# Decoder layer with a 16-expert mixture: expert gating ahead of two transposes, a 128-row scatter, low parts stored in the raw weight slots, four expert blocks loaded among the dense ones

## The reference

```python
for e in range(N_EXPERTS):
    a = jax.nn.silu(h @ w_gate[e]) * (h @ w_up[e])
    out = out + gates[..., e:e + 1] * (a @ w_down[e])
```

## Time and profile before

| | before |
|---|---|
| median of 3 runs | 578.33 us |
| profiled execution, first to last instruction (span) | 576.9 us |
| TensorE (PE) busy | 563.2 us, 98% |
| VectorE busy | 276.5 us, 48% |
| ScalarE busy | 234.9 us, 41% |
| dense part (to the first expert matmul) | 0 to 358.2 us |
| experts | 358.2 to 570.2 us |
| moved by DMA | 165.2 MB, 286 GB/s in the mean |

### The profile page before, as it was taken

One profiled execution on the slowest core, in us unless ns is written; L12 is line 12 of the kernel. 1 busy time (PEld: TensorE's weight loads), 2 busy tenths in 40 slices (PEclk: granted clock), 3 DMA queues, 4 the chain that ended last, 5 costly groups with the idle time before them and its releaser, 6 DMA issues.

```text
span 576.9 us, 7293 instructions
## 1 busy us (share of the span) xinstructions
PE 563.2 (98%) x2875; PEld 379.4 (66%) x2875; DVE 276.5 (48%) x415; ACT 234.9 (41%) x314; POOL 20.8 (4%) x15
## 2 busy tenths in 40 slices
PE   8999999999998999999999999999999999999995
PEld 7889888888876778888888786434444434443333
DVE  4463686976588653997765627311222221220002
ACT  6664673584594555833655643211111111111112
POOL 0000000050010000000100120000000000000000
PEclk9999999999999999999999999999999999999998
DMA  8994674566633338656656798999999999999962
GB/s 306 406 302 151 217 258 147 196 252 208 219 110 110 110 103 310 240 157 213 198 167 198 282 427 348 351 425 425 426 428 425 427 425 426 427 425 427 425 282 75
DMA packets 46300, 165.19 MB, mean 286 GB/s; under 512 B 4276, under 2 KB 5432, under 8 KB 33720
## 3 DMA queue, kind: packets, MB, share of 16 engines
q1 hardware_dynamic: 43872, 159.12, 71.8%
q10 hardware_dynamic: 2392, 5.59, 2.8%
HBM read 163.63 MB, written 1.06 MB: 285 GB/s over the span
## 4 chain that ended last, share of the span: by engine, by line
PE 90%; DVE 3%; ACT 2%; DMA 1%; DVEq 1%; issue 1%; POOL 0%; SPq 0%
PE ps L2010 19%; PE ps L1562 15%; PE ps L1554 15%; PE ps L1555 15%; PE ps L2029 10%; PE ps L1535 5%; PE ps L2054 3%; PE ps L1926 3%; DMA w_raw<-in_w_in 1%; PE ps L1729 1%; PE ps L1703 1%; PE ps L1840 1%; PE ps L1863 1%; PE ps L1917 1%; PE ps L1617 1%
## 5 line engine op out<-in xcount | busy, mean ns | idle before, releaser
L969 DVE TENSOR_TENSOR w_lo<-w_raw,w_hi 128x2048 fp32r<-128x2048 f32 (+2 forms) x52 | 113.9, 2208 | 58.9 <-ACT w_hi L565 58.3
L1554 PE MATMUL ps<-w_hi,act_hi 128*128 128x512 f32 (+1 forms) x288 | 112.2, 392 | 0.0
L1555 PE MATMUL ps<-w_hi,act_lo 128*128 128x512 f32 (+1 forms) x288 | 110.1, 384 | 0.0
L565 ACT ACTIVATE w_hi<-w_raw 128x2048 fp32r<-128x2048 f32 (+2 forms) x52 | 95.3, 1852 | 30.3 <-PE ps L1562 25.2
L2010 PE MATMUL ps<-e_raw,xg 128*64 128x512 f32 x400 | 89.1, 596 | 0.0
L1562 PE MATMUL ps<-w_lo,act_hi 128*128 128x512 f32 (+1 forms) x288 | 70.3, 386 | 0.0
L2010 PEld LDWEIGHTS ps<-e_raw,xg 128*64 128x64 f32 x400 | 27.4, 137 | 53.4 <-issue 53.2
L1554 PEld LDWEIGHTS ps<-w_hi,act_hi 128*128 128x128 f32 x288 | 54.1, 188 | 10.9 <-issue 0.7
L1555 PEld LDWEIGHTS ps<-w_hi,act_lo 128*128 128x128 f32 x288 | 54.1, 188 | 10.0
L1562 PEld LDWEIGHTS ps<-w_lo,act_hi 128*128 128x128 f32 x288 | 52.6, 188 | 10.9 <-issue 0.7
L884 ACT ACTIVATE gu<-ps,rs_slot 128x512 f32<-128x512 f32 x16 | 11.0, 687 | 96.2 <-PE ps L2010 96.2
(11 more groups left out here) (292 smaller groups left out, 710.6 us busy)
## 6 DMA issues: line engine op xcount, KB each, us to landing
w_raw<-in_w_in SPq DMA_DIRECT2D x30, 1024.0 KB, 5.2
e_raw<-in_w_expert_gate SPq DMA_DIRECT2D x25, 1024.0 KB, 15.1
e_raw<-in_w_expert_up SPq DMA_DIRECT2D x25, 1024.0 KB, 18.0
e_raw<-in_w_expert_down SPq DMA_DIRECT2D x22, 1024.0 KB, 20.9
w_raw<-in_w_expert_down SPq DMA_DIRECT2D x10, 1024.0 KB, 22.5
w_raw<-in_w_expert_gate SPq DMA_DIRECT2D x7, 1024.0 KB, 13.2
w_raw<-in_w_expert_up SPq DMA_DIRECT2D x7, 1024.0 KB, 16.2
w_raw<-in_w_xkv SPq DMA_DIRECT2D x4, 1024.0 KB, 5.1
```

Of the source, the lines that this page charges most:

```text
L565: A(bview(w_hi, b, blocks[b].shape), bview(w_raw, b, blocks[b].shape), ACT.Copy).then_inc(hi_done, 1)
L969: V.tensor_tensor(bview(w_lo, b, sh), bview(w_raw, b, sh), f32(bview(w_hi, b, sh)), ALU.subtract).then_inc(lo_done, 1)
L1554: MM(o, xh[:, t0 + k, i * P:(i + 1) * P], wh[:, k], start=first and k == 0, stop=False)
L1555: MM(o, xl[:, t0 + k, i * P:(i + 1) * P], wh[:, k], start=False, stop=False)
```

## The change

Four edits.

1. **Low parts over raw blocks.** `w_lo` has no memory of its own any more: it is written over the raw block in its slot. So the load of block b has to wait until TensorE has used block b-4.
2. **Four expert blocks early.** The 32 KB for each partition that this frees become four slots `e_early`; expert blocks 0 to 3 are loaded behind dense blocks 10 to 13.
3. **Gating ahead of the transposes.** The host writes gate and up weights in a new order, as four blocks of 1 MB for each expert, so that one PSUM bank holds gate in its left 256 columns and up in its right 256, for both halves of the tokens' columns. ScalarE applies silu to the left half (with the token's scale), VectorE multiplies by the right half, and TensorE makes two transposes in place of four; VectorE then copies the result to `a_st`.
4. **Scatter over 128 rows.** High and low part of one column half lie in one tile (`y_side`), so 4 matmuls over 128 rows take the place of 8 over 64. ScalarE and VectorE make them in two instructions each, of 64 partitions. The last expert scatters as before.

```diff
-        w_lo_at = place["at"]
-        w_lo = sb("w_lo", [P, RING, BLK], f32r)
+        w_lo = at("w_lo", w_raw_at, [P, RING, BLK], f32r)
+        e_early = sb("e_early", [P, RING, BLK])
...
                 if b >= RING:
-                    sp.wait_ge(hi_done, split_count(b - RING))
-                    sp.wait_ge(lo_done, split_count(b - RING))
+                    sp.wait_ge(mm_done, b - RING + 1)
...
             for b in range(8, NB1):
                 weight_block(b)
+                if b in EARLY:
+                    expert_load(b - EARLY[0])
...
-            for n in range(NB2):
+            for n in range(RING, NB2):
...
-                    A(y_hi[:], ps[:, 3, :], ACT.Copy, scale=w_).then_inc(s["y_hi_done"], 1)
+                    for w in range(2):
+                        A(y_side[w][side(w)], ps[side(w), 3, :], ACT.Copy, scale=w_[side(w)]).then_inc(s["y_hi_done"], 1)
...
             def gate_silu(r, e):
-                act.wait_ge(s["gu_turned"], r * NE + (e + 1))
-                A(e_act[:], ps[:, 2, :].rearrange("p (k w c) -> p k w c", w=2, c=SLOTS)[:, :, 0], ACT.Silu).then_inc(s["gate_silu_done"], 1)
...
+                A(e_act[:], ps[:, 0, 0:FF // 2], ACT.Silu, scale=rs_slot[g % 2][:, j:j + 1]).then_inc(s["gate_silu_done"], 1)
...
+                V.scalar_tensor_tensor(a_tok[:], ps[:, 0, FF // 2:FF], rs_slot[e // EPG % 2][:, e % EPG:e % EPG + 1], e_act[:],
+                                       ALU.mult, ALU.mult).then_inc(s["gu_moved"], 1)
...
+                V.tensor_copy(a_st[:].rearrange("p k c -> p (k c)"), ps[:, 2, 0:FF // 2]).then_inc(s["a_ready"], 1)
...
-                for f in range(FF // P):
-                    ins = turn(ps[:, 2, f * P:(f + 1) * P], gu[:, f:FF:FF // P], P)
+                for c in range(2):
+                    ins = turn(ps[:, 2, c * P:(c + 1) * P], a_tok[:, c * P:(c + 1) * P], P)
...
-                        for y in (y_hi, y_lo):
+                        if n is None:
                             for w in range(2):
...
+                                ins = MM(ps[:, 4 + 2 * i + w, :], selT[g % 2][:, j, i * P:(i + 1) * P], y_side[w][:], start=False,
+                                         stop=False, skip_group_check=True)
```

More of the change, by code:

```diff
@@ L49 @@
 E_RING, E_FIRST = 16, 18
+EARLY = range(10, 14)
 W_HI_ORDER = (2, 3, 0, 1)
@@ L157, in build_program @@
         m_at = region(POST + 8192)
[L158 removed]
+        assert not any(v % LINE for v in (w_hi_at, w_raw_at, act_at, q_at, zq_at, zo_at, zqk_at, zv_at, zg_at, tg_at, m_at))
         zif_at = region(NT * 8 * 4)
@@ L353, in build_program @@
             if e < NE:
-                expert_block += [(e, which, half) for half in range(2) for which in ("gate", "up")]
+                expert_block += [(e, "gu", q) for q in range(4)]
             if e:
@@ L359, in build_program, with used @@
         assert NB2 % E_RING == 0
-        def used(e, which, half):
-            return NB1 + block_at[e, which, half] + 1
+        def used(e, which, part):
+            return NB1 + block_at[e, which, part] + 1
         def split_count(b):
@@ L441, in e_slot @@
             turns = n // ring + 1 + (len(range(k, NB2, E_FIRST)) if later else 0)
[L442 to L446, removed]
+            earlier = list(EARLY_LANDED.values()) + [0] * (8 - RING) + list(LOADED.values())
+            before_ = earlier[k] if k < len(earlier) else 0
+            return e_raw[k], e_in_slot[k], before_ + 16 * turns
         SCATTERS = 2 * NE + 3
@@ L501, in _, with expert_load @@
                  (router_b[:], d_in["router_b"].rearrange("(o n) -> o n", o=1).to_broadcast([P, NE])))
+            def expert_load(n, later=False):
+                e, which, part = expert_block[n]
+                raw, landed, _ = e_slot(n, later)
+                if which == "gu":
+                    sp.dma_start(raw[:, :], d_in["w_gate_up"][e, part]).then_inc(landed, 16)
+                else:
+                    src = d_in["w_expert_down"][0, e].rearrange("(p t) n -> p t n", t=FF // P)[:, 2 * part:2 * part + 2, :]
+                    sp.dma_start(raw[:, :].rearrange("p (t n) -> p t n", t=2), src).then_inc(landed, 16)
             for b in range(8, NB1):
                 weight_block(b)
[L505 to L513, removed]
-            for n in range(NB2):
+                if b in EARLY:
+                    expert_load(b - EARLY[0])
+            for n in range(RING, NB2):
                 if n >= E_FIRST:
@@ L1458, in expert_round @@
                     more = g < NG - 1
-                    if more and j >= 2:
-                        for t in range(2 if e == 2 else 4 * j - 8, 4 * j - 4):
-                            gather_out(r, g + 1, t)
+                    tiles = range(2 if e == 2 else 4 * j - 8, 4 * j - 4) if more and j >= 2 else ()
                     if e == 0:
@@ L1979, in next_gather, with landed @@
                 gather_tile(g, t, next_bank(g, t))
-            def landed(r, e, which, half):
+            def landed(r, e, which, part):
                 later = r is not FIRST
-                raw, arrived, count = e_slot(block_at[e, which, half], later)
+                raw, arrived, count = e_slot(block_at[e, which, part], later)
                 if later:
@@ L2006, in gate_up @@
                     pe.wait_ge(s["gu_moved"], r * NE + e)
[L2007 to L2012 removed]
+                for q in (2 * half, 2 * half + 1):
+                    raw = landed(r, e, "gu", q)
+                    for t in range(2):
+                        for w in range(2):
+                            ins = MM(ps[side(w), 0, :], xg[g % 2][:, 2 * q + t, j, :], raw[:, (2 * t + w) * COLS:(2 * t + w + 1) * COLS],
+                                     start=q == 0 and t == 0, stop=q == 3 and t == 1)
+                    ins.then_inc(mm_done, 1)
             def down(r, e, half):
```

88 lines of the change are left out of this document (49 added, 39 removed).

## The result

The changed kernel takes 591.43 us, the median of four runs (589.43, 590.79, 592.08, 593.18), against 578.47 for the kernel before: slower, ratio 1.0225 with an interval of 1.0201 to 1.0249. That is 13.0 us where 8.0 were forecast. The profiled execution is the fastest of the four: 589.43 us, span 587.5, which is 10.6 above the span before.

The account below looks back on a forecast made before the run. TensorE was taken as the bound, in the experts too. Span 576.9 + 13.7 (dense part) - 5.7 (experts) = 584.9 us; the median, 1.4 above the span, gives 586.3, range 580.5 to 592.

Parts of the forecast that it names:

- block 11, `zif`: Dense part: block 11 lands later, so ScalarE moves `zif` late for TensorE, 1.0 us lost.
- branch projections: Blocks 38 to 41: late landing taken at 233.5, VectorE with hardly a gap, `tg` late; 3.5 us, bounds 2.2 and 5.
- output projection: Block 48: load, split, multiplication and `x_res` take longer than the two blocks of cover, 1.0 us lost.
- before block 50 (`mg_lo`): Not among the costed places; everywhere else the chain was called covered, so no loss.
- query projection: Block 53: `xq` ready at 320.1 where TensorE turned it at 317.38, 2.7 us lost.
- experts: Expert part: fewer transposes -3.5, scatter -2.5, down's split +0.3, together -5.7 us (between -3 and -6.5).
- four expert loads cost 0, at most 1: Early expert loads behind blocks 10 to 13: queue has room, cost 0, at most 1 us; gain 0.
- Units 3, 4 and 7: Attention, blocks 33, 34 and 36: late splits delay work ahead of `pT`; 2.8, 0.5 and 2.2 us lost.
- The clock: Rival: the granted clock falls in three of TensorE's new gaps, time 594.4 us; 6 in 100.
- The transposes' edit: Experts: two transposes less for each, 32 x 0.11 = 3.5 us saved.
- The scatter's: Experts: four matmuls of 0.23 us replace a scatter of 1.12; 2.5 us saved, 0 to 3.0, less 0.3 for down's split.
- The expert stream: Rival: expert weight loads bound the kernel, so four blocks less save 9.8 us, time 568.5; 3 in 100.

Follow-up runs that it names:

- no_early: The changed kernel with the four expert loads moved from behind dense blocks 10 to 13 to behind block 53: 592.23 us.
- wait_only: The kernel before with one edit, the load of dense block b waits until TensorE has used block b-4: 594.81 us, ratio 1.0284.
- dense_only: The kernel before with low parts over raw blocks, the later load waits and four early expert blocks, experts as before: 596.25 us, ratio 1.0312.
- experts_only: The kernel before with only the experts' edits (gating ahead of two transposes, scatter over 128 rows), dense part as before: 571.89 us, ratio 0.9892.
- ten_freed: `wait_only` with the loads of ten blocks (11, 33, 34, 36, 38 to 41, 48, 53) released by the splits as before: 578.49 us.
- reordered: The changed kernel, same memory, waits and early loads, with the late splits placed behind the work that TensorE misses: 576.29 us, ratio to before 0.9974.
- branch_order: The changed kernel with the split of block 38 behind ya and yc and, on VectorE, the first branch sum: 590.66 us.
- mem_later: The changed kernel with the 2 MB for the cross-attention's memory asked for behind the high part of block 38, not ahead: 591.7 us.
- scatter_only: The kernel before with one edit, the scatter over 128 rows, its parts made in two instructions each: 575.33 us against 578.28.

## Why the prediction was right and wrong

The sign, the places and the mechanism of the dense part were right; the size was 5 us too small. In the experts the total was right and the reason given for the scatter was not. In the order of the prediction's steps, by the shift of TensorE's block ends in the profiled execution:

| place | term | measured |
|---|---|---|
| block 11, `zif` | 1.0 | 1.7 |
| unit 3 | 2.8 | 2.9 |
| unit 4 | 0.5 | 0.4 |
| unit 7 | 2.2 | 2.4 |
| branch projections | 3.5 | 5.3 |
| output projection | 1.0 | 1.7 |
| before block 50 (`mg_lo`) | 0 | 0.7 |
| query projection | 2.7 | 2.2 |
| behind it | 0 | 0.6 |
| dense part | 13.7 | 17.9 |
| experts | -5.7 | -5.7 |

`mg_lo` is the low part of the normed activations that feed the query projection.

- **Block 11.** The term took a landing after 4.9 us; it was 5.7, where block 11 takes 5.3 in `no_early` and 5.0 in `wait_only`. The step "four expert loads cost 0, at most 1" held its bound; `no_early` puts the price at 0.5, at the one place where I had found room enough.
- **Units 3, 4 and 7.** Right to 0.2 us each. The step that a TensorE already waiting for `pT` has nothing to spare is what made them sure.
- **Branch projections.** 5.3 for 3.5: 2.9 are TensorE's later start of block 38, 1.7 that this block then takes 7.3 us and not 5.6 (the piece at half clock), and 0.7 are lost further on. Three steps were off. The landing was taken at 233.5, with 235 as the late bound, so 6.2 us after the issue with 7.6 for a bound; it took 7.5. My statement that VectorE has hardly a gap from there on was too hard: after the first `tg` only 0.7 us were lost further on, not 2.1. These two nearly cancel (2.9 for 1.4, 0.7 for 2.1), so that without the clock 3.6 would have stood against 3.5: that is luck. And the clock's 1.7 was no part of the sum.
- **Output and query projections.** 1.7 for 1.0, since block 48 landed after 5.6 us and not 4.9. 2.2 for 2.7, with 0.7 lost at `mg_lo` between them. In the prediction that place was "covered". That loss falls between the issue of block 53's load and its use, so it gives the later work that much more cover: 2.7 less 0.7 is near the 2.2 measured.
- **The clock.** This was a rival at 6 in 100, and it was partly true. Stretches at half clock while TensorE worked: one in the profiled execution of the change, three in `dense_only`, four in `wait_only` and `no_early`, none in the kernel before, `experts_only`, `ten_freed` and `reordered`. In these traces each lasts 3.4 us (one in `branch_order` 6.8) and begins in the last microsecond or so of a wait of TensorE of 1.5 us or more, or up to 2.2 us after its end. The mistake was to make the rival an alternative: the gaps of the forecast and the falls behind them come together, so a share of its price belonged into the sum. My bar for it was also wrong: I compared the gaps with 3 us at full clock behind TensorE's last matmul, and waits of 1.8 and 2.0 us were followed by a fall in some executions.
- **Experts.** The total of the expert part is exact, 5.7; the way to it is not. The transposes' edit gave 3.8 where 3.5 stood: 4.0 at the transposes themselves (7.6 to 3.6), less 0.2 beside them. The scatter's gave 1.9 where 2.5 less 0.3 stood: 2.3, less 0.4 at the last but one expert. But the reason given for it, four matmuls of 0.23 in place of 1.12 us, covers only 0.5 of that: the group stays at 1.0 to 1.1 us, and most of the gain is in the work directly ahead of it, for which the prediction had no term. So the scatter's number came near by luck. The Trainium skill ("TensorEngine Tiling (Array Packing)", Theoretical Speedup) states up to twice the speed where a dimension of at most 64 is tiled; by that, merging two tiled halves gives nothing, and the groups agree nearly (0.5 us in 15 experts).
- **The expert stream** is out as a bound: the expert part takes 206.3 us in `experts_only` and after the change alike.

The sum closes: 17.9 less 0.8 (TensorE's first blocks end 0.8 us earlier, as in all kernels here with the scatter over 128 rows) less 5.7 less 0.8 at the end are 10.6, the difference of the spans. What lies around the span is 0.5 us more than before (1.9 against 1.4). The median is 2.0 us above the profiled execution, where all runs before lie within 0.9 us; the other three runs of the change have lower mean clocks (0.994, 0.989, 0.992 against 0.995). That these 2 us are falls of the clock is not shown: only the one execution has a trace, and of the other three the slowest is not the one with the lowest clock. So the 5 us that were missing are 1.7 for the fall of the clock in this execution, 2.5 for late landings, `mg_lo` and what lies behind the query projection, and some 2 in the other runs, less about 1 at the start, the end and around the span.

## What to carry to other kernels

When a load is made to wait for the use of a slot and not for its release, count the blocks of cover, but look first at what stands *behind* the load's consumer on its in-order engine: ten of 50 late loads held the whole loss here, and moving their splits behind the work that TensorE misses got 15 us of it back without touching a single wait. When a split is moved, follow it on both engines and ask of each what it now stands in front of. And halves of a change should be timed apart: the good half, -6.1 us, was hidden by the other.

## What the runs showed of the hardware

- The granted clock doesn't fall at every wait of the same length: waits of 3.1 and 2.2 us in units 3 and 7 were each followed by a fall in `no_early`, and by none after the change. The same program's runs scatter by some 4 us, and mostly the lower clock goes with the longer time: in `mem_later` runs with a mean clock of 0.994 took 590.6 and 591.0 us, those with 0.987 took 593.9 and 594.2. It doesn't in every case: after the change the run with 0.989 took 592.1 us, the one with 0.992 took 593.2.
- From issue to landing, 1 MB took 4.9 to 5.7 us in the dense blocks from 42 on after the change, so the 4.8 to 5.4 of the earlier trace rows was too narrow, and 7.5 beside 2 MB that another engine had asked for; the last of those 2 MB took 9.7 us in `mem_later`. The Trainium skill ("DMA: Bandwidth & Descriptors", Bandwidth) gives 6.15 us for 1 MB, measured there for transfers that GpSimd issued; none of these landings from block 42 on was as long.
- What stands directly ahead of the scatter costs less when the scatter runs over 128 rows and not 64. In `scatter_only` four transposes ahead of a scatter took 0.50 us to its start, 0.68 before, and eight gather matmuls ahead of one mostly 1.02, 1.12 before; transposes ahead of a gather took 0.40 to 0.51 us in both. Why is not settled by these runs.
